# A recurrence in another order: loras and key norms behind the state steps, roots side by side, keys a lap ahead, and a wait of GpSimd moved

## The reference

```python
def step(state, inp):
    r_t, w_t, k_t, v_t, kk_t, a_t = inp
    sa = jnp.einsum('bhvk,bhk->bhv', state, kk_t)
    state = (state * w_t[:, :, None, :]
             - sa[..., None] * (kk_t * a_t)[:, :, None, :]
             + v_t[..., None] * k_t[:, :, None, :])
    y = jnp.einsum('bhvk,bhk->bhv', state, r_t)
    return state, y
...
w_log = -jax.nn.softplus(-(w0 + jnp.tanh(xw @ w1) @ w2)) - 0.5
decay = jnp.exp(-jnp.exp(w_log.astype(jnp.float32)))
a = jax.nn.sigmoid(a0 + (xa @ a1) @ a2)
g = jax.nn.sigmoid(xg @ g1) @ g2
kk = k * k_k
k = k * (1 + (a - 1) * k_a)
kk_h = kk_h / jnp.maximum(jnp.sqrt(jnp.sum(kk_h * kk_h, axis=-1, keepdims=True)), 1e-12)
y = wkv7_scan(r_h, w_h, k_h, v_h, kk_h, a_h)
y = ((y - mean) * lax.rsqrt(var + GN_EPS)).reshape(B, S, D)
bonus = (jnp.sum(r_h * k_h * r_k.astype(jnp.float32), axis=-1, keepdims=True) * v_h).reshape(B, S, D)
out = ((y + bonus).astype(h.dtype) * g)
```

## Time and profile before

| | us |
|---|---|
| median of three runs (lowest, highest) | 3166.33 (3158.36, 3174.09) |
| the profiled execution | 3160.19 |
| its span | 3158.4 |
| TensorE busy in the span | 2863.1 |
| laps 0 to 8 in the span | about 1786 to 2249 |

### The profile page before, as it was taken

One profiled execution on the slowest core, in us unless ns is written; L12 is line 12 of the kernel. 1 busy time (PEld: TensorE's weight loads), 2 busy tenths in 40 slices (PEclk: granted clock), 3 DMA queues, 4 the chain that ended last, 5 costly groups with the idle time before them and its releaser, 6 DMA issues.

```text
span 3158.4 us, 63151 instructions
## 1 busy us (share of the span) xinstructions
PE 2863.1 (91%) x24206; PEld 2582.4 (82%) x24206; DVE 1977.4 (63%) x2576; ACT 1473.1 (47%) x2011; POOL 134.8 (4%) x160
## 2 busy tenths in 40 slices
PE   2399999899999999975999899989889999999998
PEld 2399998788888898975888677777788888889998
DVE  6878887876676666678564354544347666665444
ACT  0143443476766633338454232322346666665333
POOL 0000000000000000000000221211000000000000
PEclk8599999999999999997999899999899999999999
DMA  8788887666665678862565355444435555655653
GB/s 290 262 293 277 299 300 274 229 193 189 190 186 187 194 248 282 288 220 74 166 198 176 123 174 167 158 145 165 133 125 166 186 186 186 186 186 174 186 168 127
DMA packets 506154, 628.07 MB, mean 199 GB/s; under 512 B 26392, under 2 KB 434824, under 8 KB 505736
## 3 DMA queue, kind: packets, MB, share of 16 engines
q1 hardware_dynamic: 501952, 622.62, 60.5%
q10 hardware_dynamic: 4040, 3.07, 0.3%
HBM read 623.50 MB, written 2.10 MB: 198 GB/s over the span
## 4 chain that ended last, share of the span: by engine, by line
PE 76%; DVE 10%; DMA 7%; ACT 3%; issue 3%; ACTq 0%; DVEq 0%; SPq 0%
PE ps L1809 26%; PE ps L1793 21%; PE ps L1812 14%; PE ps L1990 9%; DMA raw<-in_ffn_w_out 5%; DVE macc L1184 3%; DVE wlo L1163 2%; PE ps L2039 2%; ACT whi L754 1%; PE ps L1835 1%; PE ps L1826 1%; DVE mx L1500 1%; DMA raw<-in_fox_w_in 1%; PE ps L1898 1%; DMA crow<-in_ffn_conv_b 0%
## 5 line engine op out<-in xcount | busy, mean ns | idle before, releaser
L1163 DVE TENSOR_TENSOR wlo<-raw,whi 128x1024 fp32r<-128x1024 f32 x792 | 966.1, 1228 | 721.0 <-ACT whi L754 719.5
L754 ACT ACTIVATE whi<-raw 128x1024 fp32r<-128x1024 f32 x792 | 832.1, 1059 | 928.4 <-PE ps L1812 310.6
L1809 PE MATMUL ps<-xs,whi 128*128 128x512 f32 x3328 | 1172.5, 397 | 18.5 <-DVE xs L1247 10.8
L1812 PE MATMUL ps<-xs,wlo 128*128 128x256 f32 x3328 | 936.5, 281 | 0.0
L1809 PEld LDWEIGHTS ps<-xs,whi 128*128 128x128 f32 x3328 | 627.5, 189 | 167.3 <-issue 11.6
L1793 PE MATMUL ps<-act,whi 128*128 128x256 f32 x3840 | 708.3, 287 | 38.0 <-DVE wlo L1163 37.7
L1793 PEld LDWEIGHTS ps<-act,whi 128*128 128x128 f32 x3840 | 608.2, 195 | 45.3 <-DVE wlo L1163 45.0
L1812 PEld LDWEIGHTS ps<-xs,wlo 128*128 128x128 f32 x3328 | 632.5, 190 | 0.0
L1793 PE MATMUL ps<-act,wlo 128*128 128x256 f32 x1920 | 548.5, 286 | 0.0
L1793 PEld LDWEIGHTS ps<-act,wlo 128*128 128x128 f32 x1920 | 374.1, 195 | 0.0
L1184 DVE SCALAR_TENSOR_TENSOR macc<-raw,cact,macc 128x1024 f32<-128x1024 f32 (+1 forms) x252 | 294.0, 1167 | 6.0 <-DMA raw<-in_mod_w 1.8
(11 more groups left out here) (262 smaller groups left out, 3024.1 us busy)
## 6 DMA issues: line engine op xcount, KB each, us to landing
raw<-in_ffn_w_in SPq DMA_DIRECT2D x352, 512.0 KB, 3.6
raw<-in_mod_w SPq DMA_DIRECT2D x288, 512.0 KB, 5.1
raw<-in_ffn_w_out SPq DMA_DIRECT2D x176, 512.0 KB, 4.6
raw<-in_fox_w_in SPq DMA_DIRECT2D x96, 512.0 KB, 5.7
raw<-in_mod_w SPq DMA_DIRECT2D x128, 384.0 KB, 4.8
raw<-in_fox_w_out SPq DMA_DIRECT2D x32, 512.0 KB, 7.3
raw<-in_rwkv_w_r SPq DMA_DIRECT2D x32, 512.0 KB, 3.4
raw<-in_rwkv_w_k SPq DMA_DIRECT2D x32, 512.0 KB, 4.6
```

The costliest lines, as they stand in the source:

```text
L754: sc.activation(whi[:, half, :, :].rearrange("p k n -> p (k n)"), slots[slot], ACT.Copy).then_inc(w_hi, 1)
L1163: v.tensor_tensor(wlo[:, half, :, :].rearrange("p k n -> p (k n)"), slots[slot], whi[:, half, :, :].rearrange("p k n -> p (k n)").bitcast( ...
L1809: pe.matmul(ps[bank + m][:, :], whi[:, half, k, m * P:m * P + P], src[:, kt, :, :].rearrange("p u s -> p (u s)"), start=kt == 0, stop=Fals ...
L1812: last = pe.matmul(ps[bank + m][:, 0:S], wlo[:, half, k, m * P:m * P + P], src[:, kt, 0, :], start=False, stop=kt == KT - 1, skip_group_ch ...
```

## The change

- **TensorE.** The lora products are split: decay and learning-rate loras run directly behind the fourth state step, the gate's behind z of level 1. The key norm's sum moves behind z of level 2, its spread behind u of level 3 next to the group norm's, which comes later too. Four of the eight pieces of the modulation move by one place, and its second sum goes behind the last u. At a lap's start the wait for the last doubled copy stands behind `rhs(0)` instead of ahead of `vtok`.
- **ScalarE.** Sigmoids come ahead of level 1's copy, the root of the key norm directly ahead of the root of the variance, exponentials behind them, the gate's copy at the end. `mfin` is copied behind z of level 2 (first half) and ahead of z of level 5 (second half).
- **VectorE.** `decays` stand ahead of level 1, `adaln_out(0)` and `kk_norm` behind level 2, the keys `b_k` of the next group behind level 4 instead of at the next lap's start, `bo`, `o` and `bonus` behind level 5.
- **GpSimd.** It no longer waits for `yc` at its first copy but at the last, that into `ut`; its copy of v comes ahead of the product with r, and it doesn't wait for the running sum.
- Banks: the key norm uses ps5 in place of ps4, the group norm's spread ps4 in place of ps5. SyncE waits for the gate's lora instead of all loras.

```diff
@@ -692,8 +692,6 @@
                     pool.wait_ge(*pr_v.at("pone"))
                 else:
                     pool.wait_ge(*pr_pe.at("ln", i - 1))
-                if not at_start(i, 0) and not at_start(i - 1, 0):
-                    pool.wait_ge(*sc_v.at("yc", i - 2))
 
                 pool.tensor_copy(pcol[:, 0, :], col[:, ds(t0 + C_KK, 2)]).then_inc(*g_.inc("c0"))
                 pool.tensor_copy(pcol[:, 1, :], hka[:, ds(t0, 2)]).then_inc(*g_.inc("c1"))
@@ -727,7 +725,9 @@
                     pool.tensor_scalar(dec[:, p, :], dec[:, p, :], pcol[:, 3, p:p + 1],
                                        None, ALU.mult).then_inc(*g_.inc(f"rk{p}"))
 
-                pool.tensor_copy(vloc[:, :, :], vfm[:, ds(t0, 2), :]).then_inc(*g_.inc("v"))
+                if not at_start(i, 0) and not at_start(i - 1, 0):
+                    pool.wait_ge(*sc_v.at("yc", i - 2))
+                    waited(pool)
                 pool.tensor_copy(ut[q][:, :, :, :, :].rearrange("p a c u s -> p (a c u) s"),
                                  i64.unsqueeze(1).broadcast_to([P, 2 * CH * 2, HD])).then_inc(*g_.inc("ui"))
 
@@ -1117,26 +1124,31 @@
                 if turn:
                     sc.wait_ge(*sc_pe.at(f"y{CH - 1}", n_))
                     sc.activation(flat(ysb), ps[6][:, :], ACT.Copy).then_inc(*sc_a.inc("y"))
+                if ahead:
+                    sigmoids(i + 1)
                 z_out(1)
                 if turn:
                     sc.wait_ge(*sc_v.at("yc", n_))
                     sc.activation(sqy[:, :, :], yc[:, :, :], ACT.Square).then_inc(*sc_a.inc("sqy"))
+                z_out(2)
+                gemv_result(0)
+                if ahead:
+                    key_norm(i + 1)
+                if turn:
                     sc.wait_ge(*sc_pe.at("var", n_))
-                    sc.activation(sd8[:, :], ps[5][:, 0:8], ACT.Sqrt, bias=eps[1], scale=1.0 / HD).then_inc(
+                    sc.activation(sd8[:, :], ps[5][:, 8:16], ACT.Sqrt, bias=eps[1], scale=1.0 / HD).then_inc(
                         *sc_a.inc("sd"))
-                gemv_result(0)
-                z_out(2)
-                if ahead:
-                    sigmoids(i + 1)
                 z_out(3)
                 if ahead:
-                    norms(i + 1, 1 - q, turn)
+                    decay_products(i + 1)
                 z_out(4)
+                gemv_result(1)
+                z_out(5)
+                if ahead:
+                    gates(i + 1, 1 - q, turn)
                 if turn:
                     sc.wait_ge(*sc_v.at("o", n_))
                     sc.activation(act[:, ds(n_ * 2, 2), 0, :], yc[:, :, :], ACT.Copy).then_inc(*sc_a.inc("hi"))
-                gemv_result(1)
-                z_out(5)
 
             chunk_laps(sc, chunk_head, chunk_lap)
             out_proj(2, ph_rwkv_out, 4, ph_up[1])
@@ -1690,8 +1703,6 @@
                             lvl[:, n, :].bitcast(I32).unsqueeze(1).broadcast_to([P, CH, P]),
                             ps[2 + p][:, :].rearrange("p (c s) -> p c s", c=CH)).then_inc(*pr_v.inc(f"u{n}p{p}"))
 
-                if prep:
-                    b_k(i)
                 state(0)
                 decayed(1)
                 masked(0)
@@ -1707,56 +1718,59 @@
                     v.copy_predicated(ut[q][:, :, :, 1, :].rearrange("p a c s -> p (a c) s"), level(0, 1, 2 * CH),
                                       both).then_inc(*pr_v.inc("tb"))
 
+                if ahead:
+                    decays(i + 1, w)
+                doubled(1, 0)
+                doubled(1, 1)
                 if turn:
                     v.wait_ge(*sc_pe.at("mean", n_))
                     v.scalar_tensor_tensor(flat(yc), ps[4][:, :], -1.0 / HD, flat(ysb), ALU.mult, ALU.add).then_inc(
                         *sc_v.inc("yc"))
-                doubled(1, 0)
-                doubled(1, 1)
+                doubled(2, 0)
+                doubled(2, 1)
+                if prep:
+                    adaln_out(ph_chunk, i, 0)
+                if ahead:
+                    kk_norm(i + 1, w)
                 if turn:
                     v.wait_ge(*sc_a.at("sd", n_))
                     v.reciprocal(sd8[:, :], sd8[:, :]).then_inc(*sc_v.inc("rd"))
                     v.wait_ge(*sc_v.at("rd", n_))
                     v.tensor_copy(sdb[:, :, :], sd8[:, :].unsqueeze(2).broadcast_to([P, 8, HD])).then_inc(
                         *sc_v.inc("rs"))
+                doubled(3, 0)
+                doubled(3, 1)
+                if turn:
                     v.wait_ge(*sc_pe.at("vx", n_))
-                    v.tensor_tensor(flat(yc), flat(yc), ps[5][:, :], ALU.mult).then_inc(*sc_v.inc("yn"))
-                doubled(2, 0)
+                    v.tensor_tensor(flat(yc), flat(yc), ps[4][:, :], ALU.mult).then_inc(*sc_v.inc("yn"))
+                if ahead:
+                    kk_r(i + 1, w)
+                    decay_r(i + 1, w)
+                doubled(4, 0)
+                doubled(4, 1)
+                if ahead:
+                    b_k(i + 1)
                 if turn:
                     v.wait_ge(*sc_v.at("yn", n_))
                     for p in range(2):
                         v.tensor_scalar(yc[:, p, :], yc[:, p, :], col[:, ds(n_ * 2 + (C_GNW + p), 1)],
                                         col[:, ds(n_ * 2 + (C_GNB + p), 1)], ALU.mult, ALU.add).then_inc(
                                             *sc_v.inc(f"gn{p}"))
-                doubled(2, 1)
+                doubled(5, 0)
+                doubled(5, 1)
                 if turn:
                     v.wait_ge(*sc_v.at("gn1", n_))
                     v.tensor_tensor(flat(yc), flat(yc), flat(bonv[w]), ALU.add).then_inc(*sc_v.inc("bo"))
                     v.wait_ge(*sc_v.at("bo", n_))
                     v.tensor_tensor(flat(yc), flat(yc), flat(gate[w]), ALU.mult).then_inc(*sc_v.inc("o"))
+                if ahead:
+                    bonus(i + 1, w)
                 if prep:
-                    adaln_out(ph_chunk, i, 0)
-                if ahead:
-                    decays(i + 1, w)
-                doubled(3, 0)
-                doubled(3, 1)
-                if ahead:
-                    kk_norm(i + 1, w)
-                    kk_r(i + 1, w)
-                doubled(4, 0)
-                doubled(4, 1)
-                if ahead:
-                    decay_r(i + 1, w)
+                    adaln_out(ph_chunk, i, 1)
                 if turn:
                     v.wait_ge(*sc_a.at("hi", n_))
                     v.tensor_tensor(act[:, ds(n_ * 2, 2), 1, :], yc[:, :, :],
                                     act[:, ds(n_ * 2, 2), 0, :].bitcast(F32), ALU.subtract).then_inc(*sc_v.inc("lo"))
-                if ahead:
-                    bonus(i + 1, w)
-                doubled(5, 0)
-                doubled(5, 1)
-                if prep:
-                    adaln_out(ph_chunk, i, 1)
 
             chunk_laps(v, chunk_head, chunk_lap)
             out_proj(2, ph_rwkv_out, ph_up[1])
@@ -1989,19 +2003,23 @@
             def small_mm(dst, lhs, rhs, start=True, stop=True):
                 return pe.matmul(dst, lhs, rhs, start=start, stop=stop, skip_group_check=True)
 
-            def loras(i, again):
+            def loras(i):
 
                 pe.wait_ge(lw_in, i * 48 + 48)
-                if again:
-
-                    pe.wait_ge(*sc_v.at("yn", i - 2))
                 for p in range(2):
                     small_mm(ps[4][:, p * S:p * S + S], lw[0:LORA, 0, p * P:p * P + P], tw[:, :])
-                    small_mm(ps[5][:, p * S:p * S + S], lw[0:LORA, 1, p * P:p * P + P], ta[:, :])
+                    last = small_mm(ps[5][:, p * S:p * S + S], lw[0:LORA, 1, p * P:p * P + P], ta[:, :])
+                last.then_inc(*hd_pe.inc("lora"))
+
+            def lora_gate(i, again):
+
+                if again:
+                    pe.wait_ge(*sc_a.at("y", i - 2))
+                for p in range(2):
...
@@ -2163,14 +2184,14 @@
                         last_.then_inc(*c_.inc(f"u{n}p{p}"))
 
                 if prep:
-                    pe.wait_ge(*pr_v.ended(i))
                     pe.wait_ge(*hd_v.at("bonv", i))
                     turned("vtok", ps[1], vloc, hd_g.at("v", i))
                 else:
-                    pe.wait_ge(*pr_v.ended(i))
                     pe.wait_ge(*sc_v.ended(n_))
                 rhs(0)
+                pe.wait_ge(*pr_v.ended(i))
                 if prep:
+                    pe.wait_ge(*hd_a.at("gate", i))
                     turned("btok", ps[2], bneg, hd_v.at("bneg", i))
                 solve(0)
                 if prep:
@@ -2206,48 +2227,54 @@
                 if prep:
                     gemv(i, 0, 2)
                 state_y(3)
+                if ahead:
+                    loras(i + 1)
+                z_mm(1)
                 if prep:
                     gemv(i, 0, 3)
-                z_mm(1)
+                if ahead:
+                    lora_gate(i + 1, turn)
+                u_mm(1)
                 if turn:
```

(39 more changed lines are left out.)

51 lines of the change are left out of this document (30 added, 21 removed).

## The result

The changed kernel took 3187.13 us (median of 4 runs, 3183.29 to 3189.23). Beside it the kernel before took 3162.4 us (median of 4). The recorded ratio is 1.006, with a 95% interval of 1.0032 to 1.0087 (the two medians alone give 1.0078): slower, by less than 1% but clear of the spread. I had said 3166, no change.

The account below looks back on a forecast made before the run. TensorE, busy 91% of the span, was taken as the bound, so only its idle time could change. Terms +2.2 - 1.0 - 3.1 + 2.0 = +0.1 us, put on the median: 3166 us, own range 3155 to 3177, 8-in-10 range 3149 to 3179.

Parts of the forecast that it names:

- the four parts: Stage: laps 1, 3, 5, 6 +2.2 us; laps 2, 4 -1.0; head and lap 0 -3.1; lap 7 and last +2.0.
- The four old waits: TensorE in an ordinary lap: waits at loras, fifth gemv piece, `sdb` and `nrb` go, all 2.90 us with the DMA's 0.11.
- Wait 2: Last level: z5's copy queues behind ScalarE's second `mfin`, which needs the eighth gemv piece; TensorE waits 1.24 us.
- wait 4: Lap's end: `vtok` waits for `bonv`, now behind the last doubled copies, `bo` and `o`: 1.95 us where 0.89 stood.
- the jump hiding wait 4: Behind laps 2 and 4: TensorE's 4.3 us of standing at the loop jump hide wait 4, so -0.5 us each.
- lap 7 and the last: Last lap's first step waits 2.8 us for `lo` of lap 7; lap 7 itself -0.8; +2.0 us in sum.
- the tables: ScalarE: 17 table loads instead of 16, 1.28 us each, none on the path: 0 us.
- Wait 3: Eighth gemv piece waits for its DMA into the buffer the sixth gives back: 0.15 us, at least 0, about 1 if late.
- Wait 1: At `adaln_sum(0)`: `mfin` is copied behind `z_out(2)`, which stands behind `sqy`; TensorE waits 1.0 us.
- The head and lap 0: Earlier root in the head -0.6 us, lap 0's end 2.5 us earlier; together -3.1, between 0 and -4.
- only waits change: Whole stage: no matmul is added or taken away, so the forecast counted only changes in TensorE's waits.
- rival B: Lap starts: TensorE may start at half clock behind wait 4, +7 to +12 us, 3176 us; chance 0.10.

Follow-up runs that it names:

- c0: The kernel before, unchanged, measured and profiled again as a control: 3164.4 us, ratio 1.0006.
- c1: The changed kernel, unchanged, measured and profiled again as a control: 3189.3 us, ratio 1.0084 to the kernel before.
- e1: Changed kernel with TensorE's wait for `bonv` moved from ahead of `vtok` to ahead of `solve(0)`: 3169.1 us, ratio 1.0013 to the kernel before.
- e2: Changed kernel with the sixth gemv piece behind u3 instead of z4, and z5 copied ahead of the second `mfin`: 3160.7 us, 0.999 to the kernel before.
- e6: Kernel before with VectorE's `bonus` behind the last two doubled copies instead of ahead of them: 3166.0 us, ratio 1.0013.
- e4: Changed kernel with `adaln_sum(0)` behind u2, the variance sum behind z3 and its root behind `z_out(3)`: 3162.5 us, ratio 1.0004 to the kernel before.
- e3: Changed kernel with the edits of e1 and e2 together: 3143.0 us, ratio 0.9927 to the kernel before.
- e8: Changed kernel with ScalarE's first `mfin` copied ahead of `sqy` and the z2 copies: 3170.6 us, ratio 1.0007 to the kernel before.
- e10: e7 plus one filler matmul of 128 columns in each of TensorE's waits for ScalarE in the last lap: 3124.0 us, ratio 0.9881 to the kernel before.
- e7: Changed kernel with the edits of e3 and e4, last lap waiting for `yn` of lap 6 instead of `lo`: 3126.4 us, 0.9881 to the kernel before.
- e11: e7 with laps 1 to 6 written out instead of a loop of three turns: 3119.3 us, ratio 0.9852 to the kernel before.
- e14: e11 plus the eight filler matmuls in the last lap: 3114.6 us, ratio 0.9831 to the kernel before.

## Why the prediction was wrong

*The sum of waits held.* I had +0.1 us; TensorE's idle time in the stage changed by +2.4 in the first pair of profiles and by -0.4 between the means of two. In part that is luck: the four parts, forecast at +2.2, -1.0, -3.1 and +2.0, came out at +0.7, +0.8, -1.3 and +2.3.

*Terms that were right.* The four old waits went. Wait 2 (1.24 said, 1.07 measured), wait 4 (1.95, 1.71), the jump hiding wait 4 (4.37 against 4.35), lap 7 and the last (+2.0, +2.3), and the tables: 17 loads in the head and laps, none with a wait of TensorE behind it. Each load begins 0.02 us behind the instruction ahead of it, takes 1.28 us, and in 15 of the 17 the next function starts 0.01 us behind it; the other two waited for their input. Here the trace goes on disagreeing with the drain that the Trainium skill's "ScalarE: Activation LUTs" gives under *What ACT_TABLE_LOAD costs*. My reading that the standing at the jump counts from TensorE's own last matmul held in these two profiles only: it was 5.92 in `c0` and 2.51 in `c1`.

*Terms that were off.* Wait 3, the eighth piece's DMA: 0.15 said, 0.38 to 0.41 measured in laps 1, 3 and 5, but 1.75, 1.65 and 1.28 in laps 2, 4 and 6, above the bound of 1. I read one short pair of pieces (5.3 us) as the rule; in lap 2 it was 6.9. So laps 2 and 4 came out at +0.8 us together, not -1.0, and laps 1, 3, 5 and 6 at +0.7, not +2.2. Wait 1: 1.0 said, 0.42 measured. The head and lap 0: -3.1 said, -1.3 measured; the fourth piece's 2.73 us did go, but waits of 0.87 and 1.07 came into lap 0, and TensorE was busy 1.5 us longer at the lower clock, so that it grew from 47.74 to 48.29 us.

*The step that failed* is "only waits change". In the list of parts a microsecond of TensorE's work counted the same wherever it stood, and the clock was put into rival B, with a chance of 0.10, as something that follows wait 4. It was nearly the whole loss in the stage: busy time +14 of 16 us in the first profile, +22 of 22 in the mean, at an unchanged number of matmuls. B named one place out of two. At the starts of laps it came true: in the first profile `vtok` was at half clock in the four laps that wait 1.6 to 1.7 us for `bonv`, with 1.07 and 0.4 to 1.3 us of waiting ahead of that, and not in lap 1, which waits 0.39. Wait 4 had to be there (`e1`: none low without it), alone it brought two of four (`e2`), and at 1.38 us in the old order none that was not low before (`e6`). The other place, u2 behind the key norm and `adaln_sum(0)`, stands nowhere in the prediction. The order rows showed these two coming together, and I read them only for what they wait for. `e4` moves them apart: no fall is left behind them, TensorE's busy time in the stage is 421.5 us, and the median is 25 to 27 us lower.

The rule that I cited against lap 2's row ("TensorE: Matmul & The Clock Gate", *What's actually happening*, in the Trainium skill: the low clock is the default, activity releases it) was the better guide. I set it aside because of two rows, a fall behind 0.91 us and none behind 0.89. The runs agree with the rule: with the waits and narrow sums spread the clock is 1.00 in lap 2, with nearly the same idle time in clusters (7.8 us, before 7.4) it is 0.91. What I had drawn from it, two waits close together weigh more than four spread ones, was right; I gave it a tenth.

*The threshold.* "I am wrong if the clock is below 0.95 in laps 2, 4 and 6": it was 0.91, 0.93 and 0.96.

## What to carry to other kernels

When a change only reorders, write down next to each wait what TensorE does in the microseconds around it, other waits and matmuls of one or two columns above all. Equal sums of idle time did not cost the same here: spread in pieces of 0.3 to 1 us they mostly cost themselves, close together often the clock behind them too. Before explaining a difference between two profiles, run both kernels a second time and compare stretch by stretch, since unchanged loops here differ by 10 us from one execution to the next.

## What the runs showed of the hardware

- Matmuls of one and two columns count as busy in the profile (1.05 us for eight), and yet half clock came behind them. Two groups of them with 0.42 us between them were followed by half clock in 2 and 5 laps of six in the two profiles of the changed kernel (5, 3 and 3 in `e1` to `e3`), without the wait in 2 of six (`e8`), and with other work between them in 1 of 30 (`e10`; none in `e4`, `e7`, `e11` and `e14`).
- TensorE stood 2.2 to 5.9 us at the loop's jump, each time until 1.5 to 1.9 us behind the landing of a 16 KB transfer of instructions, and without fillers it started at half clock behind it, 26 times of 26; written out it waited 0 to 0.7 us there, and the longer code cost nothing that shows.
- How much low clock there is differs from one execution of the same kernel to the next (91 and 135 us of it, 16 us of the stage), so a profile of such a kernel is one draw.
- The same loop at full clock ran at two rates, 2309 or 2267 matmuls in 400 us, each loop and execution by itself. This stays open.
